# Query and key norms in an attention stage: the keys' mean by one block-matrix matmul, reciprocal roots by logarithm and exponential on ScalarE

## The reference

```python
def rmsnorm(x, g):
    y = xf * lax.rsqrt(jnp.mean(xf * xf, axis=-1, keepdims=True) + EPS)
    return y * g

qkv = (xn @ w_qkv).reshape(B, L, 3, N_HEADS, HEAD_DIM)   # 16 heads of 64
q = rmsnorm(qkv[:, :, 0], gq)
k = rmsnorm(qkv[:, :, 1], gk)
v = qkv[:, :, 2]
# per head: softmax(q k^T / 8 + bias, masked), then times v; then @ w_o
```

## Time and profile before

| what | value |
|---|---|
| three runs | 1864.13, 1865.4, 1860.33 us; median 1864.13 us |
| profiled execution, its own time | 1859.85 us |
| its span, first to last instruction | 1858.1 us |
| busy share of PE, DVE, ACT, POOL | 99%, 71%, 44%, 16% |
| granted TensorE clock, mean | 1.000 |
| from one pair's squares to the next, pairs 1 to 7 | about 26.2 us |

### The profile page before, as it was taken

One profiled execution on the slowest core, in us unless ns is written; L12 is line 12 of the kernel. 1 busy time (PEld: TensorE's weight loads), 2 busy tenths in 40 slices (PEclk: granted clock), 3 DMA queues, 4 the chain that ended last, 5 costly groups with the idle time before them and its releaser, 6 DMA issues.

```text
span 1858.1 us, 26529 instructions
## 1 busy us (share of the span) xinstructions
PE 1848.1 (99%) x10116; PEld 1581.6 (85%) x10116; DVE 1310.8 (71%) x2086; ACT 819.9 (44%) x1344; POOL 292.3 (16%) x247
## 2 busy tenths in 40 slices
PE   9999999999999999999999999999999999999999
PEld 7898988977688988989889898898777788989889
DVE  7686865975466867768767686686776666868666
ACT  5343443643244433435534343465655543433333
POOL 0210401203301203102021130111111002104011
PEclk9999999999999999999999999999999999999999
DMA  5244236632032222348323223662222232332356
GB/s 186 75 142 119 91 114 173 166 127 91 23 114 102 102 97 86 114 123 229 102 74 131 91 91 114 181 156 86 70 80 79 74 114 74 113 110 90 111 159 162
DMA packets 79737, 210.70 MB, mean 113 GB/s; under 512 B 15144, under 2 KB 28105, under 8 KB 79626
## 3 DMA queue, kind: packets, MB, share of 16 engines
q1 hardware_dynamic: 56800, 182.48, 28.6%
q0 software_dynamic: 9216, 16.78, 5.3%
q10 hardware_dynamic: 13610, 9.93, 1.9%
HBM read 190.29 MB, written 3.93 MB: 105 GB/s over the span
## 4 chain that ended last, share of the span: by engine, by line
PE 98%; DVE 1%; ACT 0%; DMA 0%; issue 0%; SPq 0%; ACTq 0%; DVEq 0%
PE bank L1290 25%; PE bank L1292 25%; PE bank L1291 25%; PE bank L1242 6%; PE bank L1245 5%; PE bank L1246 5%; PE bank L1402 1%; PE bank L1569 1%; PE bank L1553 1%; PE bank L1415 1%; PE bank L1393 1%; PE bank L1423 0%; PE bank L1541 0%; PE bank L1382 0%; DMA x<-in_x_tokens 0%; PE bank L1345 0%
## 5 line engine op out<-in xcount | busy, mean ns | idle before, releaser
L1290 PE MATMUL bank<-xh,whr 128*128 128x512 f32 x1408 | 551.5, 392 | 2.3 <-DVE wlr L466 1.0
L1291 PE MATMUL bank<-xl,whr 128*128 128x512 f32 x1408 | 549.1, 390 | 0.0
L1292 PE MATMUL bank<-xh,wlr 128*128 128x512 f32 x1408 | 549.0, 390 | 0.0
L457 ACT ACTIVATE whr<-rest 128x512 fp32r<-128x512 f32 (+1 forms) x445 | 273.2, 616 | 455.4 <-PE bank L1292 445.5
L466 DVE TENSOR_TENSOR wlr<-rest,whr 128x512 fp32r<-128x512 f32 (+1 forms) x445 | 323.3, 730 | 124.5 <-ACT whr L457 121.7
L1290 PE MATMUL bank<-hsh,whr 128*128 128x256 f32 x1232 | 349.1, 283 | 0.4 <-issue 0.3
L1291 PE MATMUL bank<-hsl,whr 128*128 128x256 f32 x1232 | 348.6, 283 | 0.0
L1292 PE MATMUL bank<-hsh,wlr 128*128 128x256 f32 x1232 | 348.6, 283 | 0.0
L1290 PEld LDWEIGHTS bank<-xh,whr 128*128 128x128 f32 x1408 | 265.1, 188 | 60.0 <-issue 2.1
L1292 PEld LDWEIGHTS bank<-xh,wlr 128*128 128x128 f32 x1408 | 265.0, 188 | 55.7
L1291 PEld LDWEIGHTS bank<-xl,whr 128*128 128x128 f32 x1408 | 265.1, 188 | 55.4 <-issue 1.0
(11 more groups left out here) (188 smaller groups left out, 2114.6 us busy)
## 6 DMA issues: line engine op xcount, KB each, us to landing
rest<-in_ffn_w_up SPq DMA_DIRECT2D x62, 512.0 KB, 4.7
rest<-in_ffn_w_gate SPq DMA_DIRECT2D x61, 512.0 KB, 3.8
rest<-in_ffn_w_down SPq DMA_DIRECT2D x54, 512.0 KB, 4.6
raw_area<-in_ffn_w_gate SPq DMA_DIRECT2D x26, 512.0 KB, 3.7
raw_area<-in_ffn_w_up SPq DMA_DIRECT2D x26, 512.0 KB, 4.7
raw_area<-in_ffn_w_down SPq DMA_DIRECT2D x26, 512.0 KB, 4.6
raw_area<-in_w_qkv SPq DMA_DIRECT2D x24, 512.0 KB, 3.4
rest<-rest POOLq DMA_DIRECT2D x38, 256.0 KB, 4.6
```

Source lines behind the costliest of these rows:

```text
L457: act.activation(whr[:, at:at + st.kb, :].rearrange("p k c -> p (k c)"), weights(st, buf)[:, 0, :], ACT.Copy).then_inc(high, 1)
L1290: pe.matmul(out, whr[:, at, :], hi, start=start, stop=False, skip_group_check=onto)
L1291: pe.matmul(out, whr[:, at, :], lo, start=False, stop=False, skip_group_check=onto)
L1292: return pe.matmul(out, wlr[:, at, :], hi, start=False, stop=stop, skip_group_check=onto)
```

## The change

The keys' means and their use are apart from the queries'. `heads`, a 128x128 matrix with 1/64 in the two diagonal blocks of 64x64 and zero elsewhere, is the stationary operand of one matmul with the keys' squares (512 columns): the mean of each head comes out on all of its 64 features, for each token. ACT takes the logarithm from PSUM into `rk`, and then the exponential of -0.5 times it in place; DVE multiplies `kt` with it. The queries' means are made as before, by four matmuls, but later (ahead of k=7), and their factor is a logarithm and an exponential on ACT too. The DVE reciprocal, the spreading, and the four turning matmuls are gone. `turn_values` waits for `q_ln`, the logarithm that frees bank 3, in place of `kn_done`.

```diff
@@ regions @@
-            ("rqk", [P, 2, TT, 2]), ("kwide", [P, TT, P])])
+            ("rq", [P, TT, 2]), ("lnq", [P, TT, 2]), ("rk", [P, TOK])])
@@ ACT, attention @@
                 if projects:
-                    act.wait_ge(ms_mm, p + 1)
-                    act.activation(rqk[:, :, :, :], bank[3][:, 0:4 * TT].rearrange("p (a t h) -> p a t h", a=2, t=TT),
-                                   ACT.Sqrt, bias=cst[:, C_EPS:C_EPS + 1]).then_inc(ms_std, 1)
+                    act.wait_ge(k_mean, p + 1)
+                    act.activation(rk[:, :], bank[3][:, :], ACT.Ln, bias=cst[:, C_EPS:C_EPS + 1]).then_inc(k_ln, 1)
+                    act.wait_ge(k_ln, p + 1)
+                    act.activation(rk[:, :], rk[:, :], ACT.Exp, scale=-0.5).then_inc(rk_done, 1)
                     if attends:
                         act.wait_ge(s_mm, 4 * p)
                     act.activation(qh[:, :], qt[:, :], ACT.Copy).then_inc(qh_done, 1)
+                    act.wait_ge(q_mean, p + 1)
+                    act.activation(lnq[:, :, :], bank[3][:, 0:2 * TT].rearrange("p (t h) -> p t h", t=TT), ACT.Ln,
+                                   bias=cst[:, C_EPS:C_EPS + 1]).then_inc(q_ln, 1)
+                    act.wait_ge(q_ln, p + 1)
+                    act.activation(rq[:, :, :], lnq[:, :, :], ACT.Exp, scale=-0.5).then_inc(rq_done, 1)
                     act.wait_ge(kn_done, p + 1)
                     act.activation(kh[:, :], kt[:, :], ACT.Copy).then_inc(kh_done, 1)
@@ DVE, attention @@
                     if not attends:
+                        dve.wait_ge(f_mm, 1)
+                        for h in range(2):
+                            for g in range(2):
+                                dve.memset(heads[h * HD:(h + 1) * HD, g * HD:(g + 1) * HD], 1.0 / HD if g == h else 0.0)\
+                                   .then_inc(heads_done, 1)
                         norm_factor(NORM_OF["qkv"])
...
                 if projects:
-                    dve.wait_ge(ms_std, p + 1)
-                    dve.reciprocal(rqk[:, :, :, :], rqk[:, :, :, :]).then_inc(rqk_done, 1)
-                    dve.wait_ge(rqk_done, p + 1)
-                    dve.tensor_copy(kwide[:, :, :].rearrange("p t (h c) -> p t h c", h=2),
-                                    rqk[:, 1, :, :].unsqueeze(3).to_broadcast([P, TT, 2, HD])).then_inc(kw_done, 1)
-                    dve.wait_ge(kb_mm, p + 1)
-
-                    dve.scalar_tensor_tensor(out=kt[:, :], in0=kt[:, :], scalar=gqk[:, 0:1], in1=bank[3][:, :],
+                    dve.wait_ge(rk_done, p + 1)
+                    dve.scalar_tensor_tensor(out=kt[:, :], in0=kt[:, :], scalar=gqk[:, 0:1], in1=rk[:, :],
                                              op0=ALU.mult, op1=ALU.mult).then_inc(kn_done, 1)
@@ PE, attention @@
-                def squares_mean():
-                    pe.wait_ge(sqq_done, p + 1)
+                def key_mean():
                     pe.wait_ge(sqk_done, p + 1)
+                    pe.wait_ge(heads_done, 4)
                     if attends:
                         pe.wait_ge(vs_done, p)
-                    for a_, sq in enumerate((sqq, sqk)):
-                        for t in range(TT):
-                            at = a_ * 2 * TT + 2 * t
-                            last = pe.matmul(bank[3][:, at:at + 2], sq[:, t * P:(t + 1) * P], cst[:, C_HEAD:C_HEAD + 2],
-                                             start=True, stop=True)
-                    last.then_inc(ms_mm, 1)
-
-                def key_factor(pair=p):
-
-                    pe.wait_ge(kw_done, pair + 1)
+                    pe.matmul(bank[3][:, :], heads[:, :], sqk[:, :], start=True, stop=True).then_inc(k_mean, 1)
+
+                def query_mean():
+                    pe.wait_ge(sqq_done, p + 1)
+                    pe.wait_ge(k_ln, p + 1)
                     for t in range(TT):
-                        last = pe.matmul(bank[3][:, t * P:(t + 1) * P], kwide[:, t, :], ident, start=True, stop=True)
-                    last.then_inc(kb_mm, 1)
+                        last = pe.matmul(bank[3][:, 2 * t:2 * t + 2], sqq[:, t * P:(t + 1) * P],
+                                         cst[:, C_HEAD:C_HEAD + 2], start=True, stop=True)
+                    last.then_inc(q_mean, 1)
 
                 def turn_values():
                     pe.wait_ge(evac, by["qkv"].group(p - 1, 2) + 1 + EVAC_CREDIT)
-                    pe.wait_ge(kn_done, p)
+                    pe.wait_ge(q_ln, p)
...
-                    unit(ph, 0, 2, hooks={6: squares_mean})
+                    unit(ph, 0, 2, hooks={5: key_mean, 7: query_mean})
                     return
-                if isinstance(p, int):
-                    unit(ph, p, 0, hooks={1: lambda: key_factor(0), 4: leftovers})
-                else:
-                    unit(ph, p, 0, hooks={2: leftovers})
+                unit(ph, p, 0, hooks={2: leftovers})
                 first_scores()
                 unit(ph, p, 1)
-                unit(ph, p, 2, hooks={1: second_scores, 4: first_values, 5: squares_mean, 7: key_factor})
+                unit(ph, p, 2, hooks={1: second_scores, 4: first_values, 5: key_mean, 7: query_mean})
```

More of the change, by code:

```diff
@@ L237, in build_trunk @@
         ident = cst[:, C_ID:C_ID + P]
+        heads = small[:, 5 * P:6 * P]
         def region(rows):
@@ L275, in build_trunk @@
         own.close()
-        (wh2, wl2, qt, kt, vt, sqq, sqk, vs, qh, ql, kh, kl, braw, bmask, sc, pt, oh, ol, rsum, nmax, rqk,
-         kwide) = region([
+        (wh2, wl2, qt, kt, vt, sqq, sqk, vs, qh, ql, kh, kl, braw, bmask, sc, pt, oh, ol, rsum, nmax, rq, lnq,
+         rk) = region([
             ("wh2", [P, KD, P], F32R), ("wl2", [P, KD, P], F32R), ("qt", [P, TOK]), ("kt", [P, TOK]), ("vt", [P, TOK]),
@@ L317, in build_trunk @@
         t_mm, t_done, oh_done, ol_done = sem("t_mm"), sem("t_done"), sem("oh_done"), sem("ol_done")
[L318 to L321, removed]
+        sqq_done, sqk_done, heads_done = sem("sqq_done"), sem("sqk_done"), sem("heads_done")
+        q_mean, q_ln, rq_done, k_mean, k_ln, rk_done = (sem("q_mean"), sem("q_ln"), sem("rq_done"), sem("k_mean"),
+                                                        sem("k_ln"), sem("rk_done"))
+        kn_done, v_mm, vs_done = sem("kn_done"), sem("v_mm"), sem("vs_done")
         qh_done, ql_done, kh_done, kl_done = sem("qh_done"), sem("ql_done"), sem("kh_done"), sem("kl_done")
@@ L1093, in maxima @@
                         dve.scalar_tensor_tensor(out=sc[:, h, t, :], in0=bank[4 + h % 2][:, t * SEQ:(t + 1) * SEQ],
-                                                 scalar=rqk[:, 0, 2 * s + t, a_:a_ + 1],
+                                                 scalar=rq[:, 2 * s + t, a_:a_ + 1],
                                                  in1=bmask[:, a_, (2 - 2 * t) * GRID_W:(6 - 2 * t) * GRID_W],
```

## The result

The changed kernel takes 1886.45 us (median of four runs, 1886.19 to 1888.38) against 1864.05 us of the kernel before (four runs, 1860.33 to 1865.4). The ratio is 1.0136, with a 95% interval of 1.0122 to 1.015: slower by 1.2 to 1.5% (the two medians alone give 1.012, 22.4 us). The profiled execution took 1886.19 us with a span of 1884.4 us, 26.3 us longer than the span before, and its mean granted clock is 0.995 instead of 1.000.

What follows compares the result with a forecast made beforehand. PE's issue, plus any wait reaching it, was taken as the bound: 7 x 2.2 = 15.4 us of delay, less 0.3 in turn 0, gave 15.1 us; on the shown median 1879, taken as 1878 us, range 1870 to 1887.

Steps and rivals of the forecast that it cites:

- PE's own saving, 0.9 us a turn: PE's matmuls removed less the one added: about 0.9 us less per pair, 7 us for eight, if PE never waits.
- ACT's chain: ACT from the last exponential at 1336.98 through four table loads and its activations to `pt` of head 2 at 1346.63.
- What PE meets: PE waits 0.8 us for `vt` at the next turn's unit 0, then 2.2 us for `pt` at the left-over products.
- the rival with a drain at each load: Each ACT table load holds ACT 1.38 us longer, the end 38 us later again: 1917 us; chance 0.02.
- The delay of each turn, 2.2 us: Left-over products start at 1346.65 against 1344.46, 2.2 us later after turns 1 to 7: 7 x 2.2 = 15.4 us.
- Turn 0, -0.3: After turn 0, without left-over products or a unit 0 wait for `vt`, PE keeps 0.3 us of its 0.9.
- The last pair, "changes it by a tenth": The last left-over products were 0.5 us nearer their `pt` before, said to change their delay by a tenth.
- The granted clock at 1.00: PE's clock stays at 1.00 despite the new waits, as after 2.0 us idle in one earlier stretch.
- The rival "The clock": PE, idle 2.2 us a turn, gets 1.2 GHz for the rest of unit 0: 29 us more, 1907; chance 0.05.
- The rival with a shared table: Logarithm and exponential share one ACT table, no loads within a turn: 7.1 us faster, 1857 us; chance 0.04.

Runs made afterwards that it cites:

- one table: Changed kernel, but ACT loads once, ahead of the attention stage, the set serving logarithm and exponential, with no other load in the stage: 1856.58 us, ratio 0.996.
- The kernel with the filled wait: Changed kernel with nine matmuls, results thrown away, put into PE's wait ahead of the left-over products: 1879.39 us, ratio 1.0086.
- `pt` first: Changed kernel with its four loads, but ACT makes both `pt` right after `qh`, and PE does the left-over products before the value transposes: 1861.24 us, ratio 1.0003.
- twelve matmuls: Changed kernel with twelve matmuls, results thrown away, put into PE's wait ahead of the left-over products: 1887.08 us in one run.
- three loads: Changed kernel with a single table load ahead of the stage, plus three loads per turn between `qh` and the queries' logarithm: 1880.23 us, ratio 1.0099.
- two loads at another place: Changed kernel with a single table load ahead of the stage, plus two loads per turn between the keys' logarithm and exponential: 1867.95 us, ratio 1.0033.

## Why the prediction was right in kind and short in size

The prediction was slower, 1878 us with a range of 1870 to 1887; the time is 1886.45. That it lies just inside the range is luck: the upper part stood for a slower logarithm and the spread of the runs, and neither was the reason. Against the spans, 15.1 us were forecast and 26.3 came. Of the missing 11.2, some 7.4 are the clock, and the rest are terms of the sum taken too small.

**PE's own saving, 0.9 us a turn.** Right. With one table the turns are 0.9 us shorter than before, and the first by 0.27, where 0.3 was taken.

**ACT's chain.** Right in each link. The logarithm taken as 0.69 measures 0.690, the exponential taken as 0.63 measures 0.632, the small ones 0.27 and 0.21 instead of 0.28. From the end of the last exponential to PE's start on `pt` it is 9.57 us (1313.93 to 1323.50); foretold were 9.67.

**What PE meets.** Right: the wait for `vt` is 0.53 us where 0.8 was expected, that for `pt` 2.06 to 2.09 where 2.2 was. PE reaches the products 9.81 us after the key mean instead of 7.73, so 2.08 later; 2.2 was the term. The gaps around the loads stay at 0.01 to 0.02 us, so the rival with a drain at each load did not come.

**The delay of each turn, 2.2 us.** Too small, since it ended at the start of the products. Behind it, the products take 1.50 us in place of 1.02, as they start between the two `pt`. Measured at full clock: 2.6 us. That is 0.5 in each of six turns, 3.1 us, less 0.7 for the somewhat shorter wait. The trace of the kernel before had this to read, in the last pair, where PE came just as the first `pt` was ready (ACT's two run from 1448.28 to 1449.35):

```profile
1448.91 1.57 PE L1402 MATMUL bank<-pt,vs 128*64 128x256 f32 x8
1450.41 0.50 PE L1242 MATMUL bank<-oh,whr 128*128 128x512 f32 x1
```

Those products take 1.50 us at full clock, and no row of waits shows the 0.48.

**Turn 0, -0.3.** Wrong by 0.9: with no wait for `vt` ahead of it, PE comes early to the transposes of the values and waits 0.66 us for the queries' logarithm (the single wait for `lnq` above; from start to start the transposes come 0.8 later than without it). The prediction followed `q_ln` only in the other turns, where it is not last. Without loads the -0.3 is there.

**The last pair, "changes it by a tenth".** Wrong by 0.5: the products start 9.82 us after the key mean where 7.15 were before (1441.76 to 1448.91), 2.67 later. The `pt` was nearer there, and the wait of 2.75 us is longer by what was missing in margin.

These make 15.1 - 0.7 + 3.1 + 0.9 + 0.5 = 18.9 us. The kernel with the filled wait, which has all but the clock, is slower by 17.4 us in the medians and 20.1 in the profiled spans; in the stretch of the stage given with that run it is 208.3 - 189.5 = 18.8, the rest being ahead of the stage.

**The granted clock at 1.00.** This is the step that failed. The rival "The clock" held the mechanism, at a chance of 0.05; and its price of 29 us was as wrong, since it let the lower clock last for a whole unit in every turn. What the runs show is four or five turns of six, and 1.3 to 1.6 us in each; in the turn shown, 0.35 on the products and 0.2 on each of six matmuls. From the profile: the four long turns are together 6.0 us above the 28.85 of full clock. Behind the last wait the products take 1.92 us, 0.4 above 1.50. With the 18.9 that makes 25.3 of the 26.3 measured; the last 1.0 falls behind those products, where the clock is 0.65 in the window up to 1477.9., one idle stretch in which the clock held, were read as evidence against; the changed kernel has such turns too (1294.50 to 1299.00), beside others with the same wait where it doesn't hold. One sample could not tell, and all the runs together show it: that very wait of 1.97 us for the last `pt` stands in each of the eleven profiles, and in three of them (one table, `pt` first, twelve matmuls) the clock falls behind it. The window of the earlier trace rows also ends at 1463, 0.74 us after the wait, while in the turn shown above the clock is 1.00 for the first 1.0 us behind the wait (1323.50 to 1324.50) and 0.54 in the next (to 1325.50). In the kernel before it stays at 1.00 after 1463 too.

**The rival with a shared table** came out at the time it was given, 1857 against 1856.58, but only in a kernel that loads the set itself. That the compiler's order had separate loads was read rightly.

What stays open is what decides in which turns the clock falls. Idle times of 2.06 to 2.09 us were followed by it in nine of twelve turns of the changed kernel's two profiles, 2.75 us in one of two, 0.8 and 1.47 together in four of six, 1.97 in three of eleven. A single one of 1.54 to 1.58 was followed by it once in seven, and 1.14 to 1.17 never in twelve. That something beside the wait's length differs between turns was seen, not explained.

## What to carry to other kernels

Before two functions of ACT alternate in a loop, look in the compiled order for its table loads, add each at 1.28 us to the chain in which it stands, and see whether one set serves both or whether work that others wait for can go ahead of the loads; here the first was worth 30 us and the second 25. Follow a delay past the point where the waiting engine restarts: a consumer that starts on the first of two inputs is paced by the second. And when a change makes TensorE idle again and again for about 2 us, price the matmuls behind each wait at the lower clock as well, even if the trace has one such stretch without it.

## What the hardware did that was not expected

The granted clock fell after idle times as short as 0.80 and 1.47 us in one turn (three loads), and once after a single one of 1.58 (two loads at another place). In the changed kernel it was back at 1.00 within 4.5 us of work; the same wait of 2.07 us kept it in one turn and was followed by 0.62 in the next. Nine matmuls whose results nobody reads, put into such a wait, gave some 7 us back over seven waits (1886.45 to 1879.39).
